# Two bursts of modulation weights in each attention land in places of their own beside a ring of four

## The reference

```python
for l in range(DEPTH):                                   # once with c_ctx, once with c
    sm, cm, gm, sf, cf, gf = modulation(c, mod_w[l], mod_b[l])   # silu(c) @ mod_w[l] (2048 x 12288), cut in six
    h = rms_norm(x, norm_mix_pre[l]) * (1 + cm) + sm
    q_a, k_a, v_a, q_b, k_b, v_b, u_c, v_c = split_projection(h, w_in[l])     # 2048 x 4608
    o_a = ...attention(q_a, k_a, v_a, ...)               # 6 heads; the latent sequence also reads cached keys
    o_b = ...attention(q_b, k_b, v_b, ..., sink_b[l])    # 6 query heads, 2 key heads
    o_c = chunk_gmlp(u_c, v_c, ...)                      # 4 groups of 128
    x = x + gm * rms_norm(merge_heads(o_a, o_b, o_c, w_out[l]), norm_mix_post[l])
    x = ffn_sublayer(x, sf, cf, gf, ...)                 # SwiGLU, width 5632
```

## Time and profile before

| what | value |
|---|---|
| time, median of 3 runs | 2339.31 us (2339.07 to 2342.21) |
| time of the profiled execution | 2339.66 us |
| its span, first to last instruction | 2337.9 us |
| PE busy | 2256.9 us, 97% of the span |
| DVE, ACT, POOL busy | 1623.0, 985.3, 66.0 us |
| moved by DMA | 609.91 MB, mean 261 GB/s |
| mean clock granted to PE | 0.991 of full |
| share of DMA mraw<-in_mod_w in the chain that ended last | 5% |

### The profile page before, as it was taken

One profiled execution on the slowest core, in us unless ns is written; L12 is line 12 of the kernel. 1 busy time (PEld: TensorE's weight loads), 2 busy tenths in 40 slices (PEclk: granted clock), 3 DMA queues, 4 the chain that ended last, 5 costly groups with the idle time before them and its releaser, 6 DMA issues.

```text
span 2337.9 us, 27817 instructions
## 1 busy us (share of the span) xinstructions
PE 2256.9 (97%) x10614; PEld 1783.4 (76%) x10614; DVE 1623.0 (69%) x1734; ACT 985.3 (42%) x1277; POOL 66.0 (3%) x96
## 2 busy tenths in 40 slices
PE   5999979999999999999999998899999999999998
PEld 3666656678888888888877886687888888888886
DVE  3555464489988889989887996557888544555455
ACT  3333243464444444334446344347444444433443
POOL 1000120000000000000000101000000000000000
PEclk9999999999999999999999999999999999999999
DMA  9899979868878878888866997766887666666664
GB/s 352 324 344 333 348 257 346 285 223 293 287 265 293 287 266 285 285 278 290 308 207 223 313 314 237 282 196 208 258 276 264 193 190 189 190 189 196 191 221 149
DMA packets 269285, 609.91 MB, mean 261 GB/s; under 512 B 19084, under 2 KB 19264, under 8 KB 267808
## 3 DMA queue, kind: packets, MB, share of 16 engines
q1 hardware_dynamic: 264832, 589.37, 75.1%
q0 software_dynamic: 4320, 18.75, 2.2%
HBM read 603.79 MB, written 5.45 MB: 261 GB/s over the span
## 4 chain that ended last, share of the span: by engine, by line
PE 86%; DMA 6%; DVE 4%; ACT 2%; issue 1%; POOL 1%; SPq 1%; POOLq 0%; DVEq 0%; ACTq 0%
PE bank_A L870 41%; PE bank_B L870 38%; DMA mraw<-in_mod_w 5%; PE bank_M L929 2%; PE bank_X L954 2%; DVE wlo L1469 1%; PE bank_M L918 1%; ACT junk L1190 1%; ACT whi L1176 0%; DVE acc L1490 0%; DMA x<-in_x_sample 0%; DVE x L1579 0%; SPq L575 0%; PE bank_M L859 0%; PE bank_A L1054 0%
## 5 line engine op out<-in xcount | busy, mean ns | idle before, releaser
L1469 DVE TENSOR_TENSOR wlo<-raw,whi 128x1024 fp32r<-128x1024 f32 x724 | 880.2, 1222 | 589.6 <-ACT whi L1176 588.9
L1176 ACT CAST whi<-raw 128x1024 fp32r<-128x1024 f32 x724 | 759.4, 1051 | 1164.9 <-PE bank_A L870 578.0
L870 PE MATMUL bank_B<-whi,xt_lo 128*128 128x512 f32 x1104 | 433.3, 392 | 0.0
L870 PE MATMUL bank_A<-whi,xt_lo 128*128 128x512 f32 x1088 | 429.1, 394 | 3.7 <-DVE xt_lo L1520 3.7
L870 PE MATMUL bank_B<-wlo,xt_hi 128*128 128x512 f32 x1104 | 429.9, 389 | 0.0
L870 PE MATMUL bank_B<-whi,xt_hi 128*128 128x512 f32 x1104 | 429.8, 389 | 0.0
L870 PE MATMUL bank_A<-wlo,xt_hi 128*128 128x512 f32 x1088 | 425.1, 391 | 0.0
L870 PE MATMUL bank_A<-whi,xt_hi 128*128 128x512 f32 x1088 | 424.9, 390 | 0.0
L1490 DVE SCALAR_TENSOR_TENSOR acc<-mraw,cond,acc 128x1024 f32<-128x1024 f32 x300 | 371.2, 1279 | 0.0
L870 PEld LDWEIGHTS bank_A<-whi,xt_lo 128*128 128x128 f32 x1088 | 205.1, 189 | 64.5 <-issue 22.3
L870 PEld LDWEIGHTS bank_B<-whi,xt_lo 128*128 128x128 f32 x1104 | 207.2, 188 | 53.9 <-issue 10.9
(11 more groups left out here) (232 smaller groups left out, 1571.1 us busy)
## 6 DMA issues: line engine op xcount, KB each, us to landing
mraw<-in_mod_w SPq DMA_DIRECT2D x372, 512.0 KB, 5.9
raw<-in_w_gate SPq DMA_DIRECT2D x176, 512.0 KB, 4.4
raw<-in_w_up SPq DMA_DIRECT2D x176, 512.0 KB, 4.5
raw<-in_w_down SPq DMA_DIRECT2D x176, 512.0 KB, 5.0
raw<-in_w_in SPq DMA_DIRECT2D x144, 512.0 KB, 5.5
raw<-in_w_out SPq DMA_DIRECT2D x64, 512.0 KB, 5.8
z<-in_mod_w SPq DMA_DIRECT2D x8, 512.0 KB, 13.8
gate_mix<-gate_rows POOLq DMA_DIRECT2D x4, 1024.0 KB, 8.6
```

What stands on the lines that cost most here:

```text
L870: mm = pe.matmul(bank[f"{pair}{s}"][:], xs[:, k, t], w[:, kb, :], start=(k == first and n == 0), stop=(k == (nk - 1 if last is None else l ...
L1176: act.copy(weights(u * UNIT + ph)[0], raw[:, ph % RING]).then_inc(hi_ready, 1)
L1469: dve.tensor_tensor(lo, raw[:, ph % RING], hi.bitcast(F32), ALU.subtract).then_inc(lo_ready, 1)
```

## The change

In each attention the four pieces of burst 2 and the four of burst 4 no longer go through the ring. They land in these places:

| piece of the burst | burst 2 | burst 4 |
|---|---|---|
| 0 | `xt_hi` blocks 12 to 15 | the same |
| 1 | `xt_lo` blocks 12 to 15 | the same |
| 2 | `xt_hi` blocks 6 to 9 | `z` of sequence 1, columns 0 to 1023 |
| 3 | `xt_lo` blocks 6 to 9 | `z` of sequence 1, columns 2304 to 3327 |

SP issues burst 2 after the last matmul of the `w_in` projection, and burst 4 after burst 2 has been used and the transposes of sequence 1 are done. The places have four semaphores of their own, and PE waits for these. `ring_piece` skips the eight pieces, so the bursts after them use the ring as if they had not been there: burst 3 waits for burst 1 to be used, burst 5 for burst 3. `PE_AT` gives `mod_used` the count for a ring piece. The order of the issues on SP and of the steps on PE, ACT and DVE stays the same, and so does every matmul. `spare` is a name for the memory of `xt_hi`, as `gate_ffn` already is for that of `xt_lo`.

```diff
+APART_BURSTS = (2, 4)
+def apart_halves(v):
+    l = v // 6
+    return [2 * first_chunk(v) + ATT_BURST[l] + i for i in APART_BURSTS] if v in (3, 10) else []
+def apart(m, j):
+    h = 2 * m + j // 4
+    for v in MOD_PE:
+        if h in apart_halves(v):
+            return v // 6, apart_halves(v).index(h)
+    return None
+def first_chunk(v):
+    return MOD_INIT + ND * MOD_PE.index(v)
 def ring_piece(m=None, j=0, v=None, i=0):
     if v is None:
-        return m * UNIT + j + MPIECES * sum(d < vector_of(m) for d in MOD_DVE)
-    return MOD_INIT * UNIT + MPIECES * (v - 2) + i
+        h = 2 * m + j // 4
+        return (m * UNIT + j + MPIECES * sum(d < vector_of(m) for d in MOD_DVE)
+                - 4 * sum(a < h for w in MOD_PE for a in apart_halves(w)))
+    return MOD_INIT * UNIT + MPIECES * (v - 2) + i - 4 * sum(len(apart_halves(w)) for w in MOD_PE if w < v)
...
+PE_AT = {ring_piece(m, j): m * UNIT + j for m, j in pe_pieces()}
...
+        with ExitStack() as until_keep:
+            spare = sb("spare", [P, KD, 2 * P], F32, until_keep)
         xt_hi = sb("xt_hi", [P, KD, 2 * P], F32R)
...
+        def apart_place(n, j):
+            hi = spare[:].rearrange("p k t -> p (k t)")
+            lo = gate_ffn[:].rearrange("p s d -> p (s d)")
+            early = (hi, 6 * 2 * P), (lo, 6 * 2 * P)
+            late = (z[:, 1, :], Q_A), (z[:, 1, :], Q_B)
+            t, c = (((hi, 12 * 2 * P), (lo, 12 * 2 * P)) + (late if n else early))[j % 4]
+            return t[:, c:c + KB * CH].rearrange("p (t n) -> p t n", t=KB)
...
-                sp.wait_ge(mod_used, q - MPIECES * sum(ring_piece(v=v) <= q for v in MOD_DVE) + 1)
+                sp.wait_ge(mod_used, PE_AT[q] + 1)
...
+            def apart_piece(m, j, k, col):
+                l, n = apart(m, j)
+                if n == 0:
+                    sp.wait_ge(w_used, (plan.at[(l, "win")][0] + W_INC) * UNIT if l else QUARTER * ND)
+                else:
+                    sp.wait_ge(mod_used, 4 * (apart_halves(vector_of(m))[0] + 1))
+                    for step, banks in plan.at[(l, "attention")]:
+                        if step[0] == "turn" and step[1] == 1:
+                            sp.wait_ge(filled[banks[0][0]], plan.fill[banks[0]])
+                src = a["mod_w"][l, k * P:(k + 1) * P, col:col + KB * CH].rearrange("p (t n) -> p t n", n=CH)
+                sp.dma_start(apart_place(n, j), src).then_inc(apart_landed[j % 4], 16)
...
                         lv, v = divmod(vector_of(m), 6)
+                        if apart(m, j):
+                            apart_piece(m, j, ND * (m % ND) + j // 2, v * D + j % 2 * KB * CH)
+                            continue
...
                 for j in js[::2]:
+                    at = apart(m, j)
                     for i in (j, j + 1):
-                        mraw_ready(pe, ring_piece(m, i))
+                        if at:
+                            pe.wait_ge(apart_landed[i % 4], 16 * (2 * at[0] + at[1] + 1))
+                        else:
+                            mraw_ready(pe, ring_piece(m, i))
```

More of the change, by code:

```diff
@@ L125, in dve_op, with pe_pieces @@
     return (MOD_DVE.index(v) * MPIECES + i) * 2 + s
+APART_BURSTS = (2, 4)
+ATT_BURST = [1, 0]
+def apart_halves(v):
[9 more added lines that the diff above has]
+    return MOD_INIT + ND * MOD_PE.index(v)
 def ring_piece(m=None, j=0, v=None, i=0):
     if v is None:
-        return m * UNIT + j + MPIECES * sum(d < vector_of(m) for d in MOD_DVE)
-    return MOD_INIT * UNIT + MPIECES * (v - 2) + i
+        h = 2 * m + j // 4
+        return (m * UNIT + j + MPIECES * sum(d < vector_of(m) for d in MOD_DVE)
+                - 4 * sum(a < h for w in MOD_PE for a in apart_halves(w)))
+    return MOD_INIT * UNIT + MPIECES * (v - 2) + i - 4 * sum(len(apart_halves(w)) for w in MOD_PE if w < v)
+def pe_pieces():
+    return [(m, j) for m in range(MOD_INIT + ND * len(MOD_PE)) for j in range(UNIT) if not apart(m, j)]
 def vector_of(m):
     return 0 if m < MOD_INIT else MOD_PE[(m - MOD_INIT) // ND]
+PE_AT = {ring_piece(m, j): m * UNIT + j for m, j in pe_pieces()}
 BANKS = ["A0", "A1", "B0", "B1", "M", "X0", "X1", "T"]
@@ L153, in attention_steps @@
     return s
-ATT_BURST = [1, 0]
 def att_burst(l, i):
@@ L414, in build_program @@
         first_landed = [sem(f"first_landed_{i}") for i in range(2 * UNIT - RING)]
+        apart_landed = [sem(f"apart_landed_{i}") for i in range(4)]
         mod_used = sem("mod_used")
@@ L924, in mod_quarter @@
                 for j in js[::2]:
+                    at = apart(m, j)
                     for i in (j, j + 1):
-                        mraw_ready(pe, ring_piece(m, i))
+                        if at:
+                            pe.wait_ge(apart_landed[i % 4], 16 * (2 * at[0] + at[1] + 1))
+                        else:
+                            mraw_ready(pe, ring_piece(m, i))
                     k = ND * (m % ND) + j // 2
                     for c in range(ND):
-                        mm = pe.matmul(bank["M"][32 * c:32 * c + 32, :], cond[:, 2 * k:2 * k + 32],
-                                       mraw[:, ring_piece(m, j + c // 2) % RING, c % 2, :], start=(k == 0), stop=(k == KD - 1))
+                        w = apart_place(at[1], j + c // 2) if at else mraw[:, ring_piece(m, j + c // 2) % RING]
+                        mm = pe.matmul(bank["M"][32 * c:32 * c + 32, :], cond[:, 2 * k:2 * k + 32], w[:, c % 2, :], start=(k == 0), stop=(k == KD - 1))
                         if c % 2:
```

## The result

The changed kernel takes 2326.35 us (median of six), the kernel before 2340.76 beside it; the ratio is 0.9934, with a 95% interval of 0.992 to 0.9947, or 12 to 19 us off. Two more sets of runs of the same kernel gave 0.9926 (0.9913 to 0.9939) and 0.9938 (0.9925 to 0.9952). The first profiled execution took 2320.95 us with a span of 2319.2 us, 18.7 less than the span before; it is the shortest of its set.

A forecast was written before the change was run, and what follows sets the result against it. TensorE, busy 97%, was held by waits for modulation weights and the slow clock behind them. Savings of 8.8 + 6.8 - 2 (clock) = 13.6 us off 2339.66 gave 2326.1, say 2326.0; range 2321 to 2334.

The forecast's parts named there:

- saved, first attention: First attention: burst 6 starts at 346.7 instead of 355.46, 8.8 us earlier.
- saved, second attention: Second attention: same 31.9 us from burst 2 to burst 6, saving 6.8 us because burst 2 waited less there.
- Supply: Earlier issue of weight bursts: no wait for weights in bursts 2 to 5, burst 4 having the least room.
- Rival A: Transfers in flight share the engines and finish together, costing about 3 us in each attention, so 2332; chance 0.12.
- Burst 2 to burst 3: First attention: VectorE's norm_v 0 and keep 0 are late next; burst 3 starts at 322.3 instead of 326.87.
- Burst 3 to mix 2: First attention: burst 4 at 329.7, keep 0 through top 2 in 6.04 us, mix 2 at 335.5 instead of 344.26.
- turn_p 2's wait: First attention, after burst 4: turn_p 2 newly waits 0.8 us for soft 2, which ends at 332.4.
- The clock: TensorE between burst 4 and mix 2: short idles may halve the clock, costing 1 us in each attention.
- rival C: New waits keep TensorE at half clock from burst 2 to burst 6, 36 us slower, 2376; chance 0.03.
- Burst 6's own waits: End of the attention: burst 6 still waits in the ring for burst 5, so its small wait stays.
- Rival B: Output projection behind the first attention takes back its 8.8 us, leaving 5.8, so 2333.8; chance 0.09.
- Rival D: Places come free too late or SP is held elsewhere, so bursts land as before, 2339.7; chance 0.06.

The follow-up runs named there:

- only_burst4: Changed kernel, but only burst 4 lands in its own place and burst 2 goes through the ring again; 2341.29 us, ratio 0.9997 to the kernel before.
- only_burst2: Changed kernel, but only burst 2 lands in its own place and burst 4 goes through the ring again; 2326.96 us, ratio 0.9935 to the kernel before.

## Why the prediction was right, point by point

The forecast was 2326.0 us with a range from 2321 to 2334; the median is 2326.35. That these agree to 0.4 us is luck: the three sets of runs lie 3 us apart in what they save, and by its stages the change saves 16 to 17 us where the sum had 13.6, as shown below. The chain of waits behind it was right in the main. Its steps, in us from the start of burst 2 in the first attention, against the changed kernel:

| step | predicted | measured |
|---|---|---|
| burst 3 | 7.5 | 7.8 |
| burst 4 | 14.9 | 14.75 |
| turn_p 2 | 17.6, with a new wait of 0.8 | 17.2, no wait |
| mix 2 | 20.7 | 20.1 |
| burst 6 | 31.9 | 31.3 |
| saved, first attention | 8.8 | 9.4 |
| saved, second attention | 6.8 | 7.5 |
| clock, both | -2 | 0 |

*Supply.* Right: no wait for weights but 0.17 us at burst 4's second half, the place that was named as the one with the least room. The DMA engines were nearly full from 300 to 333, at 392 to 421 GB/s in most windows of 3 us and at 268 and 339 from 309 to 315, where the stores are, so mostly near the upper of the two rates taken. The Trainium skill's rule of in-order descriptors on one queue ("DMA: Bandwidth & Descriptors", Queues, rings and completion order) agrees so far as this case goes: burst 1 was used at 306.49 without a wait, though burst 2 was issued right behind it, and so was burst 3 with `w_out` behind. Rival A, which would have made these wait, is out.

*Burst 2 to burst 3.* The right successor was named, VectorE in norm_v 0 and keep 0, and at the right size (0.79 us). What was left of score 2 behind the wait took 1.1 us (321.19 to 322.28), not the 0.8 estimated, so burst 3 came 7.8 us after burst 2. One reading was wrong, though nothing rests on it: the 5.9 us named as the cost of wait and slow clock are the length of the stretch from mix 0 to burst 3 (326.87 - 320.95); without both burst 3 would have come at 321.57, so the cost is 5.3.

*Burst 3 to mix 2.* Here a term was mis-sized. From the start of keep 0 to the end of top 2, 6.04 us were taken from the earlier trace rows; the changed kernel needs 5.33 (320.45 to 325.78). The row of before held gaps in which VectorE waited for score's matmuls. So soft 2 ended at 331.45, 0.7 us sooner than forecast (counted from burst 2), and turn_p 2's wait did not come up; ScalarE's part did, with waits of 0.28 and 0.88 us.

*The clock.* This term failed: a loss of 1 us in each attention was taken, and in three profiles of the changed kernel no half-clock stretch follows bursts 2 to 5. The idle time from burst 4 to mix 2 is 0.28 + 0.88 us, not the 2.4 forecast, since the wait of turn_p 2 was missing. The rule of "TensorE: Matmul & The Clock Gate" (A second HAM failure mode: psum-queue depth-cycling) in the Trainium skill did not bear on it at waits of this size, and rival C is out. The two attentions save 16.9 us between burst 2 and burst 6, where 15.6 - 2 were forecast: the shorter chain gave 1.3 us more and the clock took 2 us less than in the sum. Burst 6's own waits, 0.8 us together, went too, against the forecast that they stay. Against this, the stretch from the first attention to the second is 0.1 to 0.7 us longer than before, and that from the second to the end 0.5 to 0.9, of which 0.4 to 0.6 is a wait for weights at the one burst in the output projection. That leaves 16 to 17; the three sets show 13.3 to 16.7 by medians and 14.5 to 17.3 by ratios, each with 3 us either way. So by the stages the sum was some 3 us too small, most of it the clock's term, and the first set's median hides it.

*Rival B*, that the output projection takes the first gain back, is out: from the end of burst 6 to burst 0 of the second layer it is 1077.6, 1077.1 and 1077.0 us in the three profiles and 1076.9 before. *Rival D* is out for the full change; in only_burst4 its second half, SyncE held elsewhere, is what happened to burst 4.

*What the prediction did not see.* It did not ask what each of the two places brings alone. By the experiments burst 2's place alone brings 14 of the 17 us of that set, and burst 4's alone nothing, because in order on SyncE it stands behind burst 3's wait. Burst 2's place does two things: it takes away burst 2's own waits (3.55 and 1.04 + 1.56 us), and it lets burst 3 and all that stands behind it go out earlier. No run separates the two; that burst 4's wait fell by 2.4 and 1.0 us in only_burst2 shows that the second is part of it.

## What to carry to other kernels

When a transfer is late, look in the issue queue for what it stands behind before giving it a buffer: a buffer helps only if its issue is reached. Here one early place for the transfer at the head of the jam brought most of the gain, while the place further back brought nothing by itself. Size the gain by the time at which the next engine becomes late, with durations cleaned of the waits that the change removes; and to know how far there is to go, run once with the transfers made light, and compare a distance inside the stage, which repeated to 0.04 us in the changed kernel, where the total varied by several.

## What the runs showed of the hardware that was not expected

Filling TensorE's waits with unread products (warm_waits) left no stretch at half clock behind them, with eight burst matmuls in 1.07 us instead of 1.62 to 1.94, yet took at most 1.9 us from one attention's distance and none from the other's.

From 315 to 333 in the first attention of the changed kernel, 512 KB transfers issued close behind one another ran at 392 to 421 GB/s in every window of 3 us, 413 on the mean; the stretch that held the stores of keys and values was slower (268 GB/s at 309 to 312). Before, the same attention reached 359 over its busiest 12 us (324 to 336). The chip had shown such a rate at the start of the kernel before, though (413 GB/s over 12 to 30 us), so the 359 of the attention was no limit of the engines; issuing earlier raised it.
